# Expert weights of a fused three-block kernel, worked out by GpSimd and the vector engine in turns

## The reference

```python
probs_g = softmax(xf @ w_group + b_group)
p_top, g_idx = top_k(probs_g, 1)
in_group = the 4 logits (xf @ w_router + b_router) of group g_idx
w_top, e_local = top_k(softmax(in_group), 2)
w_top = w_top / sum(w_top)
gates = p_top * w_top, placed at the two chosen experts
h = silu(x @ w_gate[e]) * (x @ w_up[e])
y = sum over e of (h * gates[e]) @ w_down[e]
```

## Time and profile before

| | |
|---|---|
| median of 3 runs | 1001.53 us (1001.23 to 1001.97) |
| the profiled execution | 1001.3 us |
| its span, from first to last instruction | 999.6 us |
| mean granted TensorE clock | 0.999 of full speed |
| TensorE / vector engine / ScalarE / GpSimd busy | 966.7 / 714.7 / 549.8 / 31.3 us |
| expert stages, from the branch on | about 190 to 335 us, and 481 to 628 us |
| vector engine's 184 splits (L1900) | 417.7 us, 2287 ns each |

### The profile page before, as it was taken

One profiled execution on the slowest core, in us unless ns is written; L12 is line 12 of the kernel. 1 busy time (PEld: TensorE's weight loads), 2 busy tenths in 40 slices (PEclk: granted clock), 3 DMA queues, 4 the chain that ended last, 5 costly groups with the idle time before them and its releaser, 6 DMA issues.

```text
span 999.6 us, 15243 instructions
## 1 busy us (share of the span) xinstructions
PE 966.7 (97%) x5906; PEld 840.2 (84%) x5906; DVE 714.7 (72%) x891; ACT 549.8 (55%) x608; POOL 31.3 (3%) x73
## 2 busy tenths in 40 slices
PE   8999989999999999999999999899999999999997
PEld 8978988878888789878778888689887999998886
DVE  4788877888888774536989888845566766566566
ACT  3765644567677644653677677434553644444431
POOL 7000010000000000000000000000000000000010
PEclk9999999999999999999999999999999999999999
DMA  9653325299899945521599899736351755554611
GB/s 322 212 170 126 127 72 185 86 364 348 295 328 350 357 145 167 170 85 43 170 357 349 271 344 361 264 115 200 131 189 63 244 177 168 185 193 169 234 61 43
DMA packets 151987, 205.86 MB, mean 206 GB/s; under 512 B 6896, under 2 KB 123376, under 8 KB 151920
## 3 DMA queue, kind: packets, MB, share of 16 engines
q1 hardware_dynamic: 150912, 204.24, 60.8%
q10 hardware_dynamic: 1008, 0.71, 0.2%
HBM read 203.87 MB, written 1.05 MB: 205 GB/s over the span
## 4 chain that ended last, share of the span: by engine, by line
PE 73%; DVE 11%; ACT 6%; DMA 5%; issue 4%; SPq 0%; POOL 0%; ACTq 0%; POOLq 0%; DVEq 0%
PE psum L619 70%; DVE w_lo L1900 5%; ACT w_hi L1460 3%; DMA raw<-in_w_up 3%; DMA raw<-in_w_down 1%; ACT arena L1460 1%; DMA raw<-in_attn_w_in 1%; DVE stats L2147 1%; DVE x_res L2167 1%; DVE xt_lo L1917 1%; DVE mt_lo L1917 1%; ACT mt_hi L1460 0%; PE psum L1094 0%; PE psum L1345 0%; ACT L1460 0%
## 5 line engine op out<-in xcount | busy, mean ns | idle before, releaser
L1900 DVE TENSOR_TENSOR w_lo<-raw,w_hi 128x2048 fp32r<-128x2048 f32 x184 | 417.7, 2287 | 79.5 <-ACT w_hi L1460 74.5
L1460 ACT ACTIVATE w_hi<-raw 128x2048 fp32r<-128x2048 f32 (+1 forms) x186 | 353.6, 1905 | 127.5 <-PE psum L619 61.8
L619 PE MATMUL psum<-xt_hi,w_hi 128*128 128x256 f32 x704 | 200.9, 285 | 3.7 <-DVE xt_lo L1917 1.6
L619 PE MATMUL psum<-xt_hi,w_lo 128*128 128x256 f32 x704 | 199.2, 283 | 0.0
L619 PE MATMUL psum<-xt_lo,w_hi 128*128 128x256 f32 x704 | 199.1, 283 | 0.0
L619 PE MATMUL psum<-w_hi,mt_hi 128*128 128x512 f32 (+1 forms) x448 | 174.3, 389 | 2.9 <-DVE arena L2612 1.5
L619 PE MATMUL psum<-w_hi,mt_lo 128*128 128x512 f32 (+1 forms) x448 | 171.3, 382 | 0.0
L619 PE MATMUL psum<-w_lo,mt_hi 128*128 128x512 f32 (+1 forms) x448 | 171.0, 382 | 0.0
L619 PEld LDWEIGHTS psum<-xt_hi,w_hi 128*128 128x128 f32 x704 | 135.0, 192 | 5.1 <-issue 4.8
L619 PEld LDWEIGHTS psum<-xt_hi,w_lo 128*128 128x128 f32 x704 | 135.1, 192 | 0.0
L619 PEld LDWEIGHTS psum<-xt_lo,w_hi 128*128 128x128 f32 x704 | 135.0, 192 | 0.0
(11 more groups left out here) (261 smaller groups left out, 1196.6 us busy)
## 6 DMA issues: line engine op xcount, KB each, us to landing
raw<-in_w_gate SPq DMA_DIRECT2D x64, 512.0 KB, 5.1
raw<-in_w_up SPq DMA_DIRECT2D x64, 512.0 KB, 6.2
raw<-in_w_down SPq DMA_DIRECT2D x64, 512.0 KB, 5.8
raw<-in_ffn_w_up SPq DMA_DIRECT2D x44, 512.0 KB, 4.6
raw<-in_a_w_in SPq DMA_DIRECT2D x26, 512.0 KB, 6.8
raw<-in_attn_w_in SPq DMA_DIRECT2D x24, 512.0 KB, 5.2
raw<-in_ffn_w_down SPq DMA_DIRECT2D x22, 512.0 KB, 4.2
raw<-in_w_o SPq DMA_DIRECT2D x16, 512.0 KB, 4.7
```

The costliest lines, as they stand in the source:

```text
L619: return pe.matmul(o, l, r, start=start, stop=stop, skip_group_check=skip)
L1460: return act.activation(o, i, f, **kw)
L1900: return dve.tensor_tensor(w_half(h, w_lo), w_half(h, raw), w_half(h, w_hi).bitcast(F32), ALU.subtract).then_inc(lo_split, 1)
```

## The change

GpSimd takes over the elementwise part of `weigh_experts`, the vector engine keeps the maxima and `first_of`. The two hand the work to each other with semaphores: GpSimd makes the chosen group's logits (`expert_logits`); the vector engine the first choice (`first_pick`, ahead of the branch); GpSimd the input of the exponential, the group sum and the logits without the first choice (`others_left`); the vector engine the second choice (`second_pick`), which now stands behind the branch and behind the split of half 2 (the third half); GpSimd the gates and `gated`, in eight instructions. Reciprocals become powers of -1, one sum becomes two additions, and the term -2 times the first choice becomes two subtractions. GpSimd's part stands in its program behind the powers of the mixer's norm. Semaphore `gated` and its waiter on TensorE stay as they were; the dense path waits for it too.

```diff
-        rt = sb("rt", [P, 228])
+        rt = sb("rt", [P, 232])
...
+            def weigh_experts(layer):
+                m = [r_m[:, n, :].rearrange("p (b o) -> p b o", o=1) for n in range(8)]
+                chosen = r_og.rearrange("p b (g o) -> p b g o", o=1).to_broadcast([P, 2, 4, 4])
+                pool.wait_ge(sem("group_ready"), layer + 1)
+                own.link(pool.tensor_tensor(r_t16, r_log[:, :, 4:20].rearrange("p b (g e) -> p b g e", g=4),
+                                            chosen, ALU.mult))
+                own.link(pool.tensor_tensor(r_t16[:, :, 0:2, :], r_t16[:, :, 0:2, :], r_t16[:, :, 2:4, :], ALU.add))
+                pool.tensor_tensor(r_i4, r_t16[:, :, 0, :], r_t16[:, :, 1, :], ALU.add)\
+                    .then_inc(sem("expert_logits"), 1)
+
+                pool.wait_ge(sem("first_pick"), layer + 1)
+                pool.tensor_tensor(r_e, r_i4, m[4].to_broadcast([P, 2, 4]), ALU.subtract)\
+                    .then_inc(sem("expert_log"), 1)
+                pool.wait_ge(sem("group_exp"), layer + 1)
+                own.link(pool.tensor_tensor(r_w2, r_g[:, :, 0:2], r_g[:, :, 2:4], ALU.add))
+                own.did(pool.tensor_tensor(m[2], r_w2[:, :, 0:1], r_w2[:, :, 1:2], ALU.add))
+                pool.wait_ge(sem("expert_exp"), layer + 1)
+                own.link(pool.tensor_tensor(r_e2, r_e, r_o1, ALU.subtract))
+                pool.tensor_tensor(r_e2, r_e2, r_o1, ALU.subtract).then_inc(sem("others_left"), 1)
+
+                pool.wait_ge(sem("second_pick"), layer + 1)
+                one = ones[:, 0:2].rearrange("p (b o) -> p b o", o=1)
+                own.did(pool.tensor_tensor(r_o1, r_o1, r_o2, ALU.add))
+                own.link(pool.tensor_tensor(m[7], m[6], one, ALU.add))
+                own.did(pool.tensor_tensor(r_g4, r_e, r_o1, ALU.mult))
+                own.link(pool.tensor_tensor(m[7], m[7], m[2], ALU.mult))
+                own.link(pool.tensor_tensor(m[7], m[7], neg_ones[:, 0:2].rearrange("p (b o) -> p b o", o=1), ALU.pow))
+                own.link(pool.tensor_scalar(m[7], m[7], 1.0 / ALPHA, None, ALU.mult))
+                own.link(pool.tensor_tensor(r_g4, r_g4, m[7].to_broadcast([P, 2, 4]), ALU.mult))
+                own.link(pool.tensor_tensor(r_gate, r_g4.rearrange("p b (o e) -> p b o e", o=1)
+                                            .to_broadcast([P, 2, 4, 4]), chosen, ALU.mult))
+                pool.nop().then_inc(sem("gated"), 1)
...
-            for _ in range(6):
+            for turn in range(6):
                 for b in range(TB):
                     n += 1
                     power(n, slice(b, b + 1))
+                if turn in (0, 2):
+                    weigh_experts(turn // 2)
...
-            def weigh_experts(layer):
...
+            def first_pick(layer):
+                dve.wait_ge(sem("expert_logits"), layer + 1)
                 own.link(dve.tensor_reduce(r_m[:, 4, :], r_i4, AX, ALU.max))
                 first_of(r_o1, r_i4, r_m[:, 4, :])
+                dve.nop().then_inc(sem("first_pick"), 1)
+
+            def second_pick(layer):
+                dve.wait_ge(sem("others_left"), layer + 1)
                 own.link(dve.tensor_reduce(r_m[:, 6, :], r_e2, AX, ALU.max))
                 first_of(r_o2, r_e2, r_m[:, 6, :])
+                dve.nop().then_inc(sem("second_pick"), 1)
...
                     if q == 0 and not dense:
+                        if i == 0:
+                            spl(3)
+                            second_pick(layer)
                         spl(6)
                         slot_gates()
...
                 gather(0)
-                weigh_experts(layer)
+                first_pick(layer)
                 load = dve.value_load(load_max[0:1, 0:1], min_val=0, max_val=T)
                 with dve.If(load > FAST_LIMIT):
+                    second_pick(layer)
+                    dve.wait_ge(sem("gated"), layer + 1)
```

More of the change, by code:

```diff
@@ L416, in _ @@
             sp.wait_ge(out_in, 16 * len(GATE_TILES))
+        r_log = rt[:, 0:40].rearrange("p (b e) -> p b e", b=2)
+        r_g = rt[:, 40:48].rearrange("p (b e) -> p b e", b=2)
+        r_eq = rt[:, 48:56]
+        r_cum = rt[:, 56:64]
+        r_og = rt[:, 64:72].rearrange("p (b e) -> p b e", b=2)
+        r_t16 = rt[:, 72:104].rearrange("p (b g e) -> p b g e", b=2, g=4)
+        r_e = rt[:, 104:112].rearrange("p (b e) -> p b e", b=2)
+        r_o1 = rt[:, 112:120].rearrange("p (b e) -> p b e", b=2)
+        r_o2 = rt[:, 120:128].rearrange("p (b e) -> p b e", b=2)
+        r_m = rt[:, 128:144].rearrange("p (n b) -> p n b", b=2)
+        r_g4 = rt[:, 144:152].rearrange("p (b e) -> p b e", b=2)
+        r_gate = rt[:, 160:192].rearrange("p (b g e) -> p b g e", b=2, g=4)
+        r_pos = rt[:, 192:204].rearrange("p (n g) -> p n g", g=4)
+        r_i4 = rt[:, 208:216].rearrange("p (b e) -> p b e", b=2)
+        r_e2 = rt[:, 216:224].rearrange("p (b e) -> p b e", b=2)
+        r_mx = rt[:, 224:225]
+        r_w2 = rt[:, 228:232].rearrange("p (b e) -> p b e", b=2)
         @block.gpsimd
@@ L564, in turned @@
             return psum[:, 2 * b:2 * b + 2, :].rearrange("p c (k t) -> p c k t", t=P)
[L567 to L582, removed]
         MOE_SEMS = ("perm_ready", "turned_perm", "perm_out", "gathered", "xg_hi", "xg_lo", "y_sum", "y_hi",
@@ L2316, in place_slots @@
                 place(layer, None)
-            def weigh_experts(layer):
[L2320 to L2323, removed]
+            def first_pick(layer):
+                dve.wait_ge(sem("expert_logits"), layer + 1)
                 own.link(dve.tensor_reduce(r_m[:, 4, :], r_i4, AX, ALU.max))
-                dve.tensor_tensor(r_e, r_i4, wide(r_m[:, 4, :]), ALU.subtract).then_inc(sem("expert_log"), 1)
                 first_of(r_o1, r_i4, r_m[:, 4, :])
[L2328 to L2333, removed]
+                dve.nop().then_inc(sem("first_pick"), 1)
+            def second_pick(layer):
+                dve.wait_ge(sem("others_left"), layer + 1)
                 own.link(dve.tensor_reduce(r_m[:, 6, :], r_e2, AX, ALU.max))
                 first_of(r_o2, r_e2, r_m[:, 6, :])
[L2337 to L2347, removed]
+                dve.nop().then_inc(sem("second_pick"), 1)
             def experts(layer):
@@ L2427, in experts @@
                 gather(0)
-                weigh_experts(layer)
+                first_pick(layer)
                 load = dve.value_load(load_max[0:1, 0:1], min_val=0, max_val=T)
+                at_branch = own.n
                 with dve.If(load > FAST_LIMIT):
+                    second_pick(layer)
+                    dve.wait_ge(sem("gated"), layer + 1)
                     for b in range(TB):
@@ L2436, in experts @@
                             group(i, q, True)
+                own.n = at_branch
                 with dve.Else():
```

## The result

The changed kernel takes 1010.2 us (median of 6 runs, 1008.99 to 1012.12) against 1002.05 for the kernel before on the same chip (1001.23 to 1002.94): a ratio of 1.0083, with an interval of 1.007 to 1.0096. It is 0.8% slower. The profiled execution took 1011.03 us, its span is 1009.3, where the one before had 999.6. Times without further words, from 168 to 530 us, are positions in one profiled execution each.

The account below looks back on a forecast made before the run. TensorE, busy for 97% of the span, was taken to bound the kernel. Delays of 5.5 us less 1.3 gave 4.2; 2.6 for the clock made 6.8 on 1001.3, so 1008.1, stated as 1008; range 999.5 to 1013.

Parts of the forecast that it names:

- the likeliest case: Splits hold up GpSimd's gates, TensorE stands and its clock drops; 1006 to 1013 us, chance 0.42.
- The vector engine's steps: Ahead of the branch: 0.8 us instead of 4.0; the stall before half 2 goes, splits end at 202.5.
- GpSimd's first part: Three instructions for the expert logits, startable at 179.7 and wanted at 190.3: hidden, no cost.
- The port: Splits block GpSimd's last eight instructions except at gaps; 1.7 to 2.6 us left after the splits, 2.1 taken.
- The stand: TensorE waits for `gated` before the gates' matmuls, from 200.5 to 204.6 in the first layer: 4.1 us.
- the give-back: Two later TensorE stalls in the same group vanish because splits are well ahead: 1.3 us regained.
- held up, clock kept: Rival: the gates come late but TensorE's clock doesn't drop; 4.2 us slower, 1005 to 1008, chance 0.30.
- The clock: TensorE's clock drops after the 4.1 us stall; between nothing and 2.9 us per layer, 1.3 taken, 2.6 in all.
- The two later stalls: TensorE idle times of 0.20 and 0.76 us, waiting for the product L2392, priced at 1.3 us together.
- GpSimd slips through: Rival: GpSimd's small instructions run in pauses or beside splits, `gated` before 200.5; 997 to 998.5 us, chance 0.16.
- GpSimd wins and the splits wait: Rival: GpSimd holds the port through its chain, half 3 starts 2.6 us late; 1000 to 1003 us, chance 0.12.
- the two stalls at the head of each stage: TensorE waits before half 2's matmuls and the first transpose in both expert stages; together 3.0 us.

Follow-up runs that it names:

- experiment 2: The changed kernel, but the vector engine waits for `gated` before it splits halves 3 to 5; 1003.29 us, ratio 1.0011.
- experiment 3: The changed kernel with each of the three splits after the second choice made in four instructions of 128x512; 999.55 us, ratio 0.9973.
- experiment 4: The changed kernel with the second choice right behind the first, ahead of the branch; 1002.18 us, ratio 1.0004.
- Experiment 1: The changed kernel with 18 unused filler matmuls on TensorE before it waits for the gates; 1006.39 us, ratio 1.0044.
- experiment 5: The changed kernel with GpSimd's last eight instructions back on the vector engine, behind the split of half 3; 998.46 us, ratio 0.9966.
- experiment 6: The changed kernel with both choices ahead of the branch and half 2's split in four instructions of 128x512; 999.62 us, ratio 0.9978.
- Experiment 7: The kernel before, without GpSimd: seven vector instructions ahead of the branch, half 2's split, the other fourteen behind it; 1001.69 us, ratio 1.0002.

## Why the prediction was right, and where it was not

The sign, the place and the mechanism were those of the likeliest case, and 1010.2 lies in the range, 2 us above the 1008 forecast.

**The vector engine's steps** came as written: 0.76 us for the first choice, no stall before half 2. But they came later in layer 1. The first choice ended at 191.69 instead of 191.1 and the splits at 203.30 instead of 202.5. In this execution the first choice began 0.64 us after the old chain did, while TensorE's first matmul behind the branch was only 0.19 later. The vector engine was 0.6 us late already at 168.2 us, twelve microseconds before GpSimd's first new instruction (180.40), and the same program began its first choice at 190.06 in experiment 2: a difference between executions, not the change's. GpSimd's first part, costed at nothing, cost nothing: it was done by 181.9, nine microseconds before the first choice. It too was held, by shorter vector instructions with two long inputs in SBUF, one GpSimd instruction by each:

```profile
180.72 0.55 POOL L511 TENSOR_TENSOR rt<-rt 128x16 f32<-128x16 f32 x1
181.35 0.57 POOL L512 TENSOR_TENSOR rt<-rt 128x8 f32<-128x8 f32 x1
```

```profile
180.41 1.44 DVE L2297 SCALAR_TENSOR_TENSOR x_res<-x_res,rstd,gain 128x512 f32<-128x512 f32 x2
```

**The port.** "GpSimd gets through at most at the gaps between splits" was right, and the number at each gap is now known: one. What was left of the chain was 1.77 us after the splits in layer 1 and 1.76 in layer 2, so the lower end of the bounds, not the middle of 2.1: 0.3 us too much in each layer. Two ways of reading were open, and the Trainium skill's page "SBUF — State Buffer", section "Who interferes with whom", gave the one that held: an exclusive lock for one whole instruction, to whoever issued first. On GpSimd's side the trace agrees: L527, which issued 0.08 us ahead of the split, passed in 0.20 us; L528, behind it, took 2.27. That the vector engine is blocked in its turn no run here shows: the three splits take 6.70 us with GpSimd's instructions beside them, and 6.70 in experiment 2 without. Experiments 3 and 4 agree with the same rule at another length (0.5 to 0.7 us beside pieces of 0.61) and with other instructions held.

**The stand.** Forecast 4.1 us, measured 4.49 and 3.79. The delay of the first transposes without the clock was put at 2.7 + 2.8 = 5.5; it is 3.29 (205.18 + 3.67 − 205.56) and 2.21 (5.34 − 3.13), the same 5.5, in part because the shorter chain and the later splits of layer 1 cancel. With the give-back of 1.3 the text had 4.2 us net and the case "held up, clock kept". Experiment 1 is that case, and is 4.1 us above the kernel before by the medians, 5.3 by the profiled executions.

**The clock is the step that failed in size.** "I take a little under half, 1.3 a layer, 2.6 in all": it was 2.74 and 3.13, once under and once over the upper bound of 2.9. The bound itself left something out: it counted only the twelve matmuls of half 3, but the eight for the gates ran at the low clock too. Half 3's first matmul started 1.72 us behind theirs (205.18 to 206.90), where before it had been 0.81 (201.24 to 202.05). That is 0.91 us of each layer's sum; half 3 makes the other 1.83 and 2.22. The drop itself was foreseen from the earlier trace rows. What no row showed was how long it lasts: once low, the clock stayed low for about 6.8 us (204.1 to 210.9; 6.9 in layer 2), with TensorE busy from 205.2 on, so that nine and eleven of half 3's twelve matmuls ran at half speed. A middle value between "back at once" and "all twelve" had no row behind it.

**The give-back** was put at 1.3 us and is 1.8 less 0.15, so 1.7. The two later stalls that the text named are most of it: from the first to the fourth pair of transposes it takes 17.11 us in both layers after the change, where it took 17.53 and 18.08, 1.4 less in all. The sum by the prediction's own steps, 5.5 + 5.9 − 1.7 = 9.7, is the change of the span; the forecast was 6.8, and the 2.9 between them are 3.3 too little for the clock, less 0.4 of give-back. The medians differ by only 8.1 us, 1.6 less than the two profiled executions; that the forecast lies within 2 us of the median is luck to that extent.

**The rivals.** "GpSimd slips through" needed `gated` before 200.5; it came at 205.07. Experiments 5 and 6, other kernels in which the gates are there in time, are 3.7 and 2.6 us under the kernel before, near the 3.0 to 4.5 that the text gave this case. They don't test it: in 5 the chain is on the vector engine, in 6 a split is in pieces. "GpSimd wins and the splits wait" is experiment 2, at 1003.29, just above its 1000 to 1003; it didn't occur by itself.

**What the order was worth.** The prediction put 3.0 us on the two stalls at the head of each stage. Experiment 7 removes the stall before half 2 without GpSimd and gains nothing, since the wait for the product grows from 2.2 to 4.1 us. What the vector engine hands over is worth something only if GpSimd's part is not the one TensorE waits for.

## What to carry to other kernels

Before a short chain goes to GpSimd, look at what the vector engine runs beside it. If that is a row of long instructions with two SBUF inputs, each of GpSimd's short instructions cost one of the vector engine's in all these runs, whatever its own size: multiply the length of the chain by their duration. Either hand over only the links that fall into the vector engine's pauses, or cut its long instructions into pieces, where 0.67 us of extra vector time brought `gated` 3.4 us forward (5.02 us after the start of the three splits instead of 8.47). Price a stall of TensorE of about 4 us with the clock: here two stalls, of 4.49 and 3.79 us, cost 4.1 us of the time in all and the low clock behind them 3.8 more, and matmuls of no use put into the stalls took that part back.

## What the runs showed of the hardware that was not expected

- Where nothing holds it, GpSimd's time hardly depends on size at this scale (experiment 2): 0.19 to 0.20 us for 128x2 and for 128x8, 0.24 for 128x32, but 0.71 for a power on 128x2. On the vector engine a reciprocal in that power's place takes 0.17 (experiment 5).
- The clock can fall after a much shorter stall than that of 1.70 us which left it at 1.00 in the kernel before. In experiment 4 TensorE stood for 1.22 us before the gates' matmuls at 202.01, and the windows behind show this:

```profile
203.00:204.00 1.00, 1.00 (x5) 0.83 (x5) 1.00 (x2) 1.00 (x1) 0.00 (x0) 0.75 1.01 309
204.00:206.00 2.00, 2.00 (x7) 1.52 (x6) 1.97 (x4) 0.20 (x1) 0.00 (x0) 0.50 1.03 321
206.00:207.00 1.00, 1.00 (x4) 0.81 (x3) 0.85 (x1) 0.00 (x0) 0.00 (x0) 0.54 1.07 366
```

  The clock was low for about 3.4 us, with TensorE busy when it fell, and the first transposes came at 207.35. In the second layer of the same execution a stall of 1.25 us left it at 1.00, and they came after 3.75 us. So the length of one idle time does not decide by itself; what does was not settled here.
